# New turns for the weight places, gate weights split between the last expert products, and filler products in TensorE's waits, in a four-layer decoder

## The chip, the core and the metric

The kernel runs on one core of a Trainium2 chip. The core has a matmul engine (TensorE; PE in the profile, its weight loads PEld), a vector engine (DVE), a scalar engine (ACT), GpSimd (POOL) and a sync engine (SP), which only issues transfers here. They meet through semaphores. SP's transfers go through one hardware queue and are served in the order of issue; POOL has a software queue of its own. Both use the core's 16 DMA engines. The metric is the device time of one execution in microseconds.

## What is computed

Four post-norm layers over 256 rows of 1024 float32 values:

```python
for i in range(DEPTH):                       # mixers: conv, retention, sgu, conv
    mix = (_short_conv_mixer, _retention_mixer, _sgu_mixer)[i % 3](x, ...)
    x = _layer_norm(ALPHA * x + mix, ln_g[i, 0], ln_b[i, 0])
    ffn = _moe(x, router_w, router_b, moe_w_gate[i], moe_w_up[i], moe_w_down[i])
    x = _layer_norm(ALPHA * x + ffn, ln_g[i, 1], ln_b[i, 1])
    emb = p[i] @ ple_w_proj[i]
    gate = sigmoid(x @ ple_w_gate[i] + ple_b_gate[i])
    x = x + gate * emb
```

`_moe` routes each row to 2 of 16 experts (gate and up 1024x512, down 512x1024). All experts are loaded, and each works on at most 64 gathered rows; where an expert has more, a general path (`If(crowded > 0)`) makes further rounds. With these inputs it isn't entered.

## The kernel before, in words

**Slots.** All weights arrive as 1 MB slots, [128, 2048] float32. Mixer, embedding and gate weights ("raw" slots, `A["slots"]`) are multiplied in three parts: ACT rounds a slot into `w_hi` (`split_slot`), DVE writes the rest in place as `w_lo`, and TensorE multiplies hi by hi, lo by hi and hi by lo (lines 516 to 518). There are 6 raw places and 4 high places; `split_behind(used)` splits slots up to `used + 4`. The two row tiles of x are t = 0 and 1. A slot of a rows product is 12 matmuls for one tile.

**Experts.** A layer has 96 expert slots (`STREAM`), 12 for each pair of experts, k = 0 to 95. They are multiplied unsplit (line 875). They lie in 16 places that come free after the mixer (raw, high, four of the work area, and those of the norm and bias parameters), and two used once. `expert_places` says which place each k takes; SP issues in that order and waits for each place's last reader (line 430). The places between the first 18 and the last 14 are spread evenly between a place's first and last use.

**End of the experts.** The last pair's down products are slots 92 to 95. Their two halves of y go from PSUM through ACT (`save_y`, the rounded part) and DVE (the rest), and TensorE puts them back into rows (line 885). DVE adds and normalizes tile 0 (`add_rows`, `layer_norm`: lines 1385 to 1435), TensorE transposes it (line 527), ACT and DVE save the transpose in two parts, and TensorE starts on the four gate slots: slots 0 to 2 of tile 0, then tile 1's transposes, slot 3, and tile 1. Each engine runs its own list in the written order, so `split_behind` between two steps makes the later step wait for the splits. `stop` bounds how far it may go.

**Route.** `route` on TensorE mixes the embedding's products (`embed`, 12 for a tile) with the 24 small router products (`logit`) and then waits for DVE to choose. **Convolution.** In layers 0 and 3 DVE weighs four quads (t, q) and ACT and DVE split each; the output rows product needs quad (t, 0) for slots 0 and 1 and (t, 1) for slots 2 and 3. **Clock.** `keep_running(n, bank)` makes n bfloat16 products of constants whose result nobody reads.

## Time and profile before

| | us |
|---|---|
| median of 3 runs | 1759.38 (1757.26 to 1762.88) |
| the profiled execution, device time | 1758.18 |
| its span in the profile | 1756.3 |
| TensorE busy | 1648.1 (94%) |
| DVE busy, ACT busy | 721.5 (41%), 469.0 (27%) |
| moved by DMA | 547.98 MB, mean 312 GB/s |

The chain of work that ended last is PE 75%, DVE 13%, DMA 8%, ACT 3%. Matmuls overlap, so TensorE's busy share is high even where it isn't at its peak. PEclk 1.00 is TensorE's full clock (2.4 GHz), 0.50 the lower level (1.2 GHz). Layer 0 runs its experts from 143 to 356 us of the span and its gate from 368 us; the other layers repeat this from 622, 1117 and 1499 us.

### The profile page before, as it was taken

What the parts mean: (1) busy time and instruction counts of PE and PEld (TensorE: products, weight loads), DVE (VectorE), ACT (ScalarE), POOL (GpSimd) and SP (SyncE); (2) the same over time, 40 slices, a digit from 0 to 9 for tenths busy, and PEclk for the clock granted to TensorE, in tenths of its full rate; (3) what the DMA queues carried; (4) which work ended last, traced back from release to release, by engine and by line L of the source; (5) the groups of instructions that cost most, each with busy time, mean ns of one, the idle gap of its engine ahead of it and who ended that gap; (6) DMA issues with size and microseconds to landing.
All of it is one profiled execution on the core that took longest, in us unless ns stands there. A gap on an engine that the chain in (4) does not pass through costs nothing.

```text
span 1756.3 us, 18018 instructions
## 1 busy us (share of the span) xinstructions
PE 1648.1 (94%) x7628; PEld 989.4 (56%) x7628; DVE 721.5 (41%) x1060; ACT 469.0 (27%) x549; POOL 16.8 (1%) x34
## 2 busy tenths in 40 slices
PE   7999999879999999998799999999987999999986
PEld 5874443358777743432588778544324877434325
DVE  4572111174757721111856656311117566111117
ACT  4531111044443311111444343211103451111112
POOL 0000000000000000000000000000000000000000
PEclk9989999989999999999899999999998998999998
DMA  7487999955443899999565346999995567899991
GB/s 292 177 359 302 421 420 422 419 215 190 163 189 112 354 398 421 421 421 420 211 250 195 145 172 275 408 401 420 421 420 226 197 245 307 330 422 421 421 420 56
DMA packets 77468, 547.98 MB, mean 312 GB/s; under 512 B 8640, under 2 KB 8640, under 8 KB 12608
## 3 DMA queue, kind: packets, MB, share of 16 engines
q1 hardware_dynamic: 73584, 530.95, 74.5%
q0 software_dynamic: 3792, 15.73, 2.4%
q8 instruction: 67, 1.10, 0.2%
q14 instruction: 25, 0.20, 0.0%
HBM read 545.60 MB, written 1.05 MB: 311 GB/s over the span
## 4 chain that ended last, share of the span: by engine, by line
PE 75%; DVE 13%; DMA 8%; ACT 3%; issue 1%; SPq 0%; DVEq 0%; ACTq 0%
PE psum L875 33%; PE psum L516 10%; PE psum L518 9%; PE psum L517 9%; DMA raw<-in_slots 8%; PE psum L867 4%; DVE w_lo L1360 4%; PE psum L885 3%; PE psum L527 3%; ACT w_hi L1071 2%; PE psum L802 1%; DVE work_r L1360 1%; DVE x L1428 1%; DVE stats L1386 1%; DVE x L1385 1%
## 5 line engine op out<-in xcount | busy, mean ns | idle before, releaser
L1360 DVE TENSOR_TENSOR w_lo<-raw,w_hi 128x2048 fp32r<-128x2048 f32 x120 | 271.5, 2287 | 163.7 <-ACT w_hi L1071 163.5
L516 PE MATMUL psum<-w_hi,xT_hi 128*128 128x512 f32 x704 | 283.3, 402 | 16.3 <-DVE w_lo L1360 9.5
L517 PE MATMUL psum<-w_lo,xT_hi 128*128 128x512 f32 x704 | 278.4, 395 | 0.0
L518 PE MATMUL psum<-w_hi,xT_lo 128*128 128x512 f32 x704 | 278.3, 395 | 0.0
L1071 ACT ACTIVATE w_hi<-raw 128x2048 fp32r<-128x2048 f32 x120 | 225.2, 1909 | 137.9 <-PE psum L518 102.0
L1360 DVE TENSOR_TENSOR work_r<-psum,work_r 128x512 fp32r<-128x512 f32 x84 | 56.6, 689 | 366.8 <-ACT work_r L1071 366.8
L1071 ACT ACTIVATE work<-psum 128x512 f32<-128x512 f32 x152 | 89.4, 599 | 413.2 <-PE psum L518 206.9
L875 PE MATMUL psum<-raw,xg 128*64 128x512 f32 x784 | 183.3, 598 | 0.0
L516 PEld LDWEIGHTS psum<-w_hi,xT_hi 128*128 128x128 f32 x704 | 135.1, 192 | 50.3 <-DVE xT_lo L1360 9.6
L518 PEld LDWEIGHTS psum<-w_hi,xT_lo 128*128 128x128 f32 x704 | 134.7, 191 | 29.0
L517 PEld LDWEIGHTS psum<-w_lo,xT_hi 128*128 128x128 f32 x704 | 135.3, 192 | 27.8 <-issue 0.2
L1071 ACT ACTIVATE work_r<-psum 128x512 fp32r<-128x512 f32 x84 | 48.4, 597 | 308.2 <-PE psum L875 307.1
L875 PE MATMUL psum<-expert_high,xg 128*64 128x512 f32 x504 | 120.1, 598 | 5.6 <-DMA expert_high<-in_experts 5.6
L875 PE MATMUL psum<-expert_work,xg 128*64 128x512 f32 x472 | 110.3, 597 | 0.0
L875 PEld LDWEIGHTS psum<-raw,xg 128*64 128x64 f32 x784 | 52.2, 136 | 92.6 <-issue 89.7
L516 PE MATMUL psum<-w_hi,work_r 128*128 128x512 f32 x224 | 90.7, 405 | 11.9 <-DVE work_r L1360 7.5
L1071 ACT ACTIVATE xg<-psum 128x512 f32<-128x512 f32 x64 | 38.2, 597 | 222.3 <-PE psum L867 222.3
L518 PE MATMUL psum<-w_hi,work_r 128*128 128x512 f32 x224 | 89.1, 398 | 0.0
L875 PE MATMUL psum<-raw,work 128*64 128x512 f32 x368 | 86.3, 593 | 2.8 <-DMA raw<-in_experts 2.8
L517 PE MATMUL psum<-w_lo,work_r 128*128 128x512 f32 x224 | 88.8, 396 | 0.0
L867 PEld LDWEIGHTS psum<-work_r 128*128 128x128 f32 x512 | 69.6, 201 | 26.8 <-issue 22.7
L867 PE MATMUL psum<-work_r 128*128 128x256 f32 x512 | 76.5, 299 | 2.1 <-DVE work_r L1661 2.1
(153 smaller groups left out, 1484.3 us busy)
## 6 DMA issues: line engine op xcount, KB each, us to landing
raw<-in_experts SPq DMA_DIRECT2D x144, 1024.0 KB, 14.6
raw<-in_slots SPq DMA_DIRECT2D x120, 1024.0 KB, 4.9
expert_work<-in_experts SPq DMA_DIRECT2D x96, 1024.0 KB, 15.1
expert_high<-in_experts SPq DMA_DIRECT2D x96, 1024.0 KB, 16.1
expert_bias<-in_experts SPq DMA_DIRECT2D x20, 1024.0 KB, 12.2
expert_norm<-in_experts SPq DMA_DIRECT2D x20, 1024.0 KB, 15.9
ln_par<-in_ln_g POOLq DMA_DIRECT2D x8, 512.0 KB, 8.2
ln_par<-in_ln_b POOLq DMA_DIRECT2D x8, 512.0 KB, 11.4
```

Of the source, the lines that this page charges most:

```text
L516: mm(out, lhs[0], rhs[0], start=start, stop=False)
L517: mm(out, lhs[0], rhs[1], start=False, stop=False)
L518: return mm(out, lhs[1], rhs[0], start=False, stop=stop)
L527: last = nc.tensor.transpose(psum[:, bank, i * P:(i + 1) * P], c, ident[:, :])
L802: return mm(psum[:, 4, t * NE:(t + 1) * NE], xT[a][:, j, t * P:(t + 1) * P], rw_split[b][:, j, :], start=i == 0, stop=i == 23)
L867: last = mm(psum[:, bank, j * SEQ:(j + 1) * SEQ], x_split[a][:, t, chunk], pick[:, t, Q * SEQ:(Q + 1) * SEQ], start=t + a == 0, stop=t + a ...
L875: last = mm(psum[columns(e), bank, :], lhs(j, e), w[:, 2 * j + e, :], start=start and j == 0, stop=stop and j == 1)
L885: last = mm(psum[:, bank0 + 2 * t + c, :], where[:, t * P:(t + 1) * P], what[i][:, c * NB:(c + 1) * NB], start=start and i == 0, stop=stop ...
L1071: return nc.scalar.activation(dst, src, func)
L1360: return tt(lo, whole, hi.bitcast(F), ALU.subtract)
L1385: link(stt(xs, xs, ALPHA, psum[:, 2 * t + c, :], ALU.mult, ALU.add))
L1386: step(nc.vector.bn_stats(stats[:, t, c, :], xs))
```

## The change

- **Places**: up to k = 77 each expert slot takes the place whose last reader comes first (`min(..., key=last.get)`); from k = 78 (`BORROWED`) only raw, high and work places are used, so the norm and bias places come free at k = 63 and 66. The last places are taken as raw and high in turn.
- **Gate slots**: SP issues all of them after expert slot 95 (before: the first one ahead of slot 95). ACT and DVE split the first two ahead of the last pair's first y half, the third ahead of its second half (before: one ahead of the second half on DVE and of both on ACT), and the fourth before tile 0 is saved. (Before, DVE split gate slot 1 there, and slots 2 and 3 between saving tile 0 and normalizing tile 1.)
- **TensorE's general path** is a register loop over the rounds, in place of three copies of its body.
- **Fillers**: 10 products after the experts, behind the new semaphore `general_done`, 3 after tile 0's transposes, 2 before the wait for the choice. They multiply the constants.
- **Route**: 2 of tile 1's 12 embedding products stand ahead of the router's (before: 4).
- **Convolution**: slot 0 of tile 1 comes second (before: third), and DVE weighs three quads before it splits two.
- **Start**: the identity is loaded alone, the other constants after raw slot 5, tile 1 of x after raw slot 2; POOL's first loads wait.

```diff
@@ expert_places @@
-        ending = [*reversed(raw), *reversed(high), *work]
+        ending = [v for i in (3, 2, 1, 0) for v in (raw[i + 2], high[i])] + [raw[1], raw[0], *work]
...
-        between = [(first[v] + (final.get(v, first[v] + 5 * len(ring)) - first[v]) * i / 5, v)
-                   for v in ring for i in range(1, 5)]
+        last = {place: k for k, place in at.items() if k < n_first and place in ring}
+        for k in range(n_first, EXPERT_SLOTS - len(ending)):
+            at[k] = min((v for v in ring if k < BORROWED or v in ending), key=last.get)
+            last[at[k]] = k
@@ sync @@
-            sp.dma_start(const[:, :], A["const"]).then_inc(s_const, 16)
+            sp.dma_start(ident, A["const"][:, 0:P]).then_inc(s_ident, 16)
...
-                    if n == 1:
+                    if n == 2:
                         load_x(1)
+                    if n == 5:
+                        sp.dma_start(const[:, P:], A["const"][:, P:]).then_inc(s_const, 16)
                 for k in load_order[L]:
-                    if k == EXPERT_SLOTS - 1:
-                        load(L, n_gate)
...
-                for n in range(n_gate + 1, n_gate + (6 if L + 1 < DEPTH else 4)):
+                for n in range(n_gate, n_gate + (6 if L + 1 < DEPTH else 4)):
@@ gpsimd @@
+            pool.wait_ge(slot_full[1], 16)
             pool.dma_start(p_in, ...)
+            pool.wait_ge(weights_used, 4)
             load_norm(0, 0)
@@ tensor, conv_mixer @@
-                pe.wait_ge(gT_ready[L], 2)
-                rows_slot(n, 4, tiled(gT), 0, 0, 1, mix_done)
+                pe.wait_ge(gT_ready[L], 3)
+                rows_slot(n, 4, tiled(gT), 0, 1, 0, mix_done)
                 pe.wait_ge(gT_ready[L], 4)
-                rows_slot(n, 4, tiled(gT), 0, 1, 0, mix_done)
-                for i in range(2, 4):
+                for i in range(1, 4):
                     rows_slot(n, 4, tiled(gT), 0, 0, i, mix_done)
@@ tensor, route: range(4) is range(2), range(4, 12) is range(2, 12), then @@
+                keep_running(2, 7)
@@ tensor, end of experts @@
+                pe.wait_ge(general_done, L + 1)
+                keep_running(10, 5)
                 transpose_tile(3 * L + 2, 0)
+                keep_running(3, 1)
@@ scalar, experts @@
-                split_behind(n_gate - 3)
+                split_behind(n_gate - 2)
                 save_y(PAIRS - 1, 0, 4)
+                split_behind(n_gate - 1)
                 save_y(PAIRS - 1, 1, 7)
@@ vector, experts @@
+                stop[0] = starts[L + 1][2] if L + 1 < DEPTH else n_gate + 4
+                split_behind(n_gate - 2)
                 save_y(PAIRS - 1, 0, 4)
-                stop[0] = ...
-                split_behind(n_gate - 3)
+                split_behind(n_gate - 1)
                 save_y(PAIRS - 1, 1, 7)
@@ scalar, after experts(L) @@
-                split_behind(starts[L][2] - 2)
+                split_behind(starts[L][2])
                 save_tile(3 * L + 2, 0)
-                split_behind(starts[L][2])
@@ vector, after experts(L) @@
+                dve.sem_inc(general_done, 1)
                 dve.wait_ge(ffn_done, T * L + 1)
                 add_rows(0, 1)
                 layer_norm(0, 2 * L + 1)
-                split_behind(n_gate - 2)
+                split_behind(n_gate)
                 save_tile(3 * L + 2, 0)
-                split_behind(starts[L][2])
```

On SP, at the end of layer 0's expert loads, the order was (raw<-in_slots are the gate slots and then the next layer's first two):

```order
L430 DMA expert_norm<-in_experts 128x2048
L430 DMA raw<-in_experts 128x2048 x6
L430 DMA expert_high<-in_experts 128x2048 x4
L430 DMA expert_work<-in_experts 128x2048 x3
L383 DMA raw<-in_slots 128x2048
L430 DMA expert_work<-in_experts 128x2048
L383 DMA raw<-in_slots 128x2048 x5
```

and it is now:

```order
L429 DMA raw<-in_experts 128x2048
L429 DMA expert_high<-in_experts 128x2048
L429 DMA raw<-in_experts 128x2048 x2
L429 DMA expert_work<-in_experts 128x2048 x4
L382 DMA raw<-in_slots 128x2048 x6
```

The first gate slot moved behind the last expert slot; the other five keep their turn.

On ACT, at the end of layer 0's experts (w_hi<-raw is a gate slot's split, work_r<-psum a half of y), before:

```order
L1071 ACTIVATE work<-psum 128x512 x3
L1071 ACTIVATE work_r<-psum 128x512 x2
L1071 ACTIVATE work<-psum 128x512
L1071 ACTIVATE w_hi<-raw 128x2048
L1071 ACTIVATE work_r<-psum 128x512 x2
L1289 TENSOR_LOAD flag
```

and now:

```order
L1075 ACTIVATE work<-psum 128x512
L1075 ACTIVATE w_hi<-raw 128x2048 x2
L1075 ACTIVATE work_r<-psum 128x512
L1075 ACTIVATE w_hi<-raw 128x2048
L1075 ACTIVATE work_r<-psum 128x512
L1295 TENSOR_LOAD flag
```

Three splits now stand ahead of the second half, and two ahead of the first.

On DVE, at the same place (the first row is the half of pair 6, x<-x,psum is `add_rows` of tile 0), before:

```order
L1360 TENSOR_TENSOR work_r<-psum,work_r 128x512 x2
L1360 TENSOR_TENSOR w_lo<-raw,w_hi 128x2048
L1360 TENSOR_TENSOR work_r<-psum,work_r 128x512
L1385 SCALAR_TENSOR_TENSOR x<-x,psum 128x512
L1386 BN_STATS stats<-x 128x6
```

and now:

```order
L1365 TENSOR_TENSOR work_r<-psum,work_r 128x512
L1365 TENSOR_TENSOR w_lo<-raw,w_hi 128x2048 x2
L1365 TENSOR_TENSOR work_r<-psum,work_r 128x512
L1365 TENSOR_TENSOR w_lo<-raw,w_hi 128x2048
L1365 TENSOR_TENSOR work_r<-psum,work_r 128x512
L1390 SCALAR_TENSOR_TENSOR x<-x,psum 128x512
```

Two splits moved ahead of the first half of the last y, and one stands between the halves.

## Rows read from the trace of the kernel before

**Rows 1.** The page, part 4: shares of the chain that ended last.

```profile
PE 75%; DVE 13%; DMA 8%; ACT 3%; issue 1%; SPq 0%; DVEq 0%; ACTq 0%
```

**Rows 2.** Windows: stretch, length, busy of each engine, PEclk, DMA share, GB/s.

```profile
160.00:330.00 170.00, 169.58 (x808) 66.58 (x806) 25.97 (x47) 21.50 (x36) 1.57 (x3) 1.00 1.01 421
```

**Rows 3.** SP's issues of k = 20 and 21 (start, length), and the microseconds to landing.

```profile
149.05 0.33 SPq L430 DMA_DIRECT2D expert_work<-in_experts  x1
...
expert_work<-in_experts SPq DMA_DIRECT2D x1, 1024.0 KB, 8.0
...
157.73 0.33 SPq L430 DMA_DIRECT2D raw<-in_experts  x1
...
raw<-in_experts SPq DMA_DIRECT2D x1, 1024.0 KB, 4.8
```

**Rows 4.** Timeline, layer 0's end: start, length, instruction [idle before <- releaser].

```profile
351.72 1.91 ACT L1071 ACTIVATE w_hi<-raw 128x2048 fp32r<-128x2048 f32 x1 [6.74 <-DMA raw<-in_slots]
...
354.23 1.94 PE L875 MATMUL psum<-expert_work,work 128*64 128x512 f32 x8 [1.58 <-DMA expert_work<-in_experts]
...
356.95 0.69 DVE L1360 TENSOR_TENSOR work_r<-psum,work_r 128x512 fp32r<-128x512 f32 x1
...
359.41 0.69 DVE L1385 SCALAR_TENSOR_TENSOR x<-x,psum 128x512 f32<-128x512 f32 x1 [0.45 <-PE psum L885]
...
364.77 1.97 PE L527 MATMUL psum<-const,x 128*128 128x128 f32 x8 [5.89 <-DVE x L1435]
365.30 2.29 DVE L1360 TENSOR_TENSOR w_lo<-raw,w_hi 128x2048 fp32r<-128x2048 f32 x1
...
368.24 0.79 PE L516 MATMUL psum<-w_hi,xT_hi 128*128 128x512 f32 x1 [1.50 <-DVE xT_lo L1360]
...
369.21 4.49 DVE L1360 TENSOR_TENSOR w_lo<-raw,w_hi 128x2048 fp32r<-128x2048 f32 x2 [0.43 <-ACT w_hi L1071]
...
373.62 0.68 DVE L1385 SCALAR_TENSOR_TENSOR x<-x,psum 128x512 f32<-128x512 f32 x1
...
380.29 1.32 PE L527 MATMUL psum<-const,x 128*128 128x128 f32 x8 [1.02 <-DVE x L1435]
```

**Rows 5.** Timeline of TensorE in layer 0's gate: every third matmul, twice.

```profile
369.68 0.63 PE L516 MATMUL psum<-w_hi,xT_hi 128*128 128x512 f32 x1
...
370.96 0.63 PE L516 MATMUL psum<-w_hi,xT_hi 128*128 128x512 f32 x1
...
377.07 0.39 PE L516 MATMUL psum<-w_hi,xT_hi 128*128 128x512 f32 x1
...
377.75 0.39 PE L516 MATMUL psum<-w_hi,xT_hi 128*128 128x512 f32 x1
```

**Rows 6.** Windows, as Rows 2: layer 0's gate, and layer 3's convolution.

```profile
363.50:373.80 10.30, 7.53 (x21) 5.97 (x22) 9.73 (x10) 4.79 (x4) 0.00 (x0) 0.50 0.17 71
1449.00:1452.30 3.30, 3.30 (x9) 2.52 (x9) 3.30 (x2) 0.00 (x0) 0.00 (x0) 0.50 1.02 427
```

**Rows 7.** TensorE's waits, 86 to 96 us, then 1440 to 1460: total, times, longest.

```profile
PE psum L516 <- DVE w_lo L1360: 0.9, 1, 0.9
...
PE psum L516 <- DVE w_lo L1360: 2.4, 1, 2.4
```

**Rows 8.** Timeline of TensorE in the route of layers 0 and 1.

```profile
118.84 1.90 PE L533 MATMUL psum<-const 128*128 128x512 bf16 x8
...
137.61 0.42 PE L847 MATMUL psum<-chosen,const 128*128 128x32 f32 x1
...
615.01 0.41 PE L847 MATMUL psum<-chosen,const 128*128 128x32 f32 x2 [1.71 <-DVE chosen L1636]
```

**Rows 9.** Timeline of the start.

```profile
10.16 1.91 ACT L1071 ACTIVATE w_hi<-raw 128x2048 fp32r<-128x2048 f32 x1 [2.46 <-DMA raw<-in_slots]
...
14.54 0.76 PE L516 MATMUL psum<-w_hi,xT_hi 128*128 128x512 f32 x1 [7.47 <-DVE w_lo L1360]
...
22.75 0.50 PE L516 MATMUL psum<-w_hi,xT_hi 128*128 128x512 f32 x1 [0.53 <-DVE w_lo L1360]
```

More of the change, by code:

```diff
@@ L830, in route @@
                 pe.wait_ge(mix_read, L + 1)
-                for i in range(4):
+                for i in range(2):
                     embed(1, i)
@@ L841, in route @@
                 last.then_inc(logits_done, 1)
-                for i in range(4, 12):
+                for i in range(2, 12):
                     embed(1, i)
+                keep_running(2, 7)
                 pe.wait_ge(chosen_ready, L + 1)
@@ L1002, in experts @@
                     o = over[L]
-                    for r in range(ROUNDS):
-                        pe.wait_ge(o["pick"], (T + 1) * (r + 1))
+                    with pe.Fori(0, ROUNDS) as r:
                         with pe.Fori(0, PAIRS) as p:
-                            i = PAIRS * r
+                            pe.wait_ge(o["pick"], (T + 1) * r + (T + 1))
                             wait_over(pe, L, "vector", "weighed", r, p)
@@ L1028, in experts @@
                             wait_over(pe, L, "scalar", "hT", r, p)
-                            pe.wait_ge(o["full"], 16 * (3 * i + 3) + 48 * p)
+                            pe.wait_ge(o["full"], 48 * PAIRS * r + 48 * p + 48)
                             for c in range(2):
@@ L1460, in conv_mixer, with weigh_quad @@
                 dve.wait_ge(dve_step, steps[0])
-                for k in range(4):
+                def weigh_quad(k):
                     t, q = divmod(k, 2)
@@ L1716, in experts @@
                 save_y(PAIRS - 2, 1, 6)
+                stop[0] = starts[L + 1][2] if L + 1 < DEPTH else n_gate + 4
+                split_behind(n_gate - 2)
                 save_y(PAIRS - 1, 0, 4)
-                stop[0] = starts[L + 1][2] if L + 1 < DEPTH else n_gate + 4
-                split_behind(n_gate - 3)
+                split_behind(n_gate - 1)
                 save_y(PAIRS - 1, 1, 7)
```

34 lines of the change are left out of this document (20 added, 14 removed).

## The prediction, made before the changed kernel had run

> **What bounds the kernel.** I read the chain of waits first: three quarters of it is TensorE and 8% is DMA [rows 1]. The windows then show where that 8% lies. From 160 to 330 us the DMA engines are full at 421 GB/s and TensorE's idle is 0.4 us [rows 2]; it was ahead when the stretch began and uses its lead up. A 1 MB slot takes 1.049 MB / 421 GB/s = 2.49 us to arrive. At the end of the stage TensorE starves: the last expert slot is multiplied the moment it lands, at 354.2, after 1.58 us of idle [rows 4]. So an expert stage ends when its transfers end, and the time there is moved by three things only: idle of the transfers at its head, megabytes ahead of the last slot, and the chain behind it. Everywhere else TensorE's order and its clock decide.
>
> **Start.** TensorE's first product waits until 14.54, because ACT gets slot 0 only at 10.16 [rows 9]. Ahead of that slot stand 330 KB of constants and POOL's 256 KB. From tile 0's landing (about 5.0) to slot 0's is 5.1 us, where the slot alone takes 2.49, so POOL's transfer and what goes with it cost 2.6; the constants cost some 0.6 net of the identity. Slot 0 then lands near 6.9 and the product starts near 11.3: 3.3 us. The wait of 0.53 at 22.75 goes too, since slot 2 now stands ahead of tile 1. Term: -3.8. Were POOL's load only worth its bytes (0.6 us), it would be -1.9; were slot 1's cold stretch to shorten as well, -5.
>
> **Convolution, layers 0 and 3.** Slot 1 waited for its `w_lo`, 0.9 and 2.4 us [rows 7]. Slot 0 of tile 1 needs no new slot and its quad is ready, so it fills both. The third weighing falls into DVE's wait for ACT. In layer 3 the idle of 2.4 is followed by 3.4 us at the lower clock [rows 6]; with the gap closed half of it, 1.7, goes. Term: -0.9 - 2.4 - 1.7 = -5.0, or -3.3 if the clock falls anyway.
>
> **Route.** Two embedding products fewer stand ahead of the router's. In layers 1 and 2 the choice is late by 1.71 us [rows 8] and TensorE gains 0.5, but the last expert slot's landing doesn't depend on it there (its transfers are back to back from before the route), so I count 0. In layers 0 and 3 the clock is low and TensorE comes to the choice without idle, at 137.61 [rows 8]. The same 12 products and two fillers now stand ahead of it: 8 fillers took 1.90 at the full clock [rows 8], so two take 0.5, or 0.85 at the lower one. The loads of the stage hang on the first expert product there. Term: 2 x 0.55 = +1.1; from 0 to +1.7.
>
> **Places.** In layer 0 SP issues k = 20 at 149.05, which lands 8.0 later at 157.1, but k = 21 only at 157.73, and it lands 4.8 later at 162.5 [rows 3]. It waited for the raw place's reader, k = 6; the new rule gives it the place read by k = 4, free before 154. So 5.4 - 2.5 = 2.9 us without a transfer disappear, and as the engines are full from there on, every later landing comes 2.9 sooner. The same pattern is there once in each other layer (issues at 632.11, 1153.28 and 1513.18): 1.3, 0.9 and 3.1. Call this g; the sum is 8.3. Near the end the new rule shortens distances between a place's uses to 9, but the queue then holds far more than SP's 5 us of latency, so I cost that at nothing. It would cost if the queue ran dry. The norm and bias parameters' 1.5 MB go earlier; they stay ahead of the last slot, so nothing changes for it.
>
> **End of the experts, four times.** Taking the first gate slot from ahead of slot 95 lets that land 2.49 + g earlier. But ACT now waits for gate slots 0 and 1 before it saves the first half of y, and for slot 2 before the second. They are served behind slot 95. The total ahead of gate slot 1 is unchanged: it lands at 354.2 + 2.5 - g. From there: ACT 1.91, DVE 2.29 (the split), 0.69 (half of y), 2.29, 0.69 and small gaps, 8.0 us to the second half; and 1.77 more to the add, as from 357.64 to 359.41 before [rows 4]. The add thus comes 2.5 + 9.75 = 12.2 after 354.2 where it came 5.2 after: +7.0 - g. Queued behind ACT's wait are both halves of y; TensorE's put-back, tile 0's normalization and its transposes wait for them.
>
> What comes back: counted from the add, the first gate product starts 8.8 later as before (one split still stands ahead, 365.30). Tile 1's transposes came 20.9 later, with TensorE waiting 1.02, since its normalization started only at 373.62, behind two splits of 4.49 [rows 4]. Those are gone. The normalization is ready after 16.1, and TensorE's 36 matmuls decide: at 0.68 us for three [rows 5] 8.2 us, so 17.0. That gives back 3.8. Term: 4 x (7.0 - 3.8) - 8.3 = +4.5.
>
> **Clock at the gate.** Before, the clock is at the lower level from 363.5 to 373.8 [rows 6], after 5.89 us of idle, and three matmuls take 1.28 instead of 0.68 [rows 5]: 2.5 us lost in the product. Now TensorE idles longest ahead of the first half of y (some 7 us), so the clock will fall there. The ten fillers behind `general_done` start about with the add. At the lower clock they take 4.3 us and end a microsecond before the transposes. The loss is between 0 and 2.5 per layer; I take 0.5, nearer to none, since products now run ahead of the gate where TensorE stood idle before. Term: +2.0.
>
> By the Trainium skill ("TensorE: Matmul & The Clock Gate", "HAM oscillation — how this bites in real kernels") an idle between groups of matmuls throttles the array, and the next group starts cold every time. The trace agrees for the 5.89 us gap; taken alone it would have every gate product cold as before, which is the first rival below.
>
> **The sum.** -3.8 - 5.0 + 1.1 + 4.5 + 2.0 = -1.2 us. The register loop lies in a branch that isn't taken; `general_done` costs nothing while tile 0's normalization (5.4 us from the add to the transposes) covers it. The profiled execution took 1758.18 (its span 1756.3 and 1.9 around it), 1.2 below the median. On the median: 1758.2.
>
> **Rivals.**
> - *The splits cost y and the clock isn't won back* (slower). The place is the gate product; it decides where the clock that the fillers raise has fallen again at the product, or they don't raise it. For it: the clock stayed low through tile 0's transposes and until 373.8. Against: nothing ran ahead of them then, and fillers do now. Price 4 x 2.5 = 10 instead of 2: 1766.
> - *The places win nothing* (slower), because the short distances at the end leave the queue dry for as long as the head gained: g = 0, 1766.5. For it: 9 instead of 14 slots. Against: landings trail issues by nearly 30 us there.
> - *More is won on TensorE's side*: start -5, route 0, no cold gate product at all, 2 us less of the last terms: 1752 to 1753. For it: each bound is open. Against: all must go together.
> - *Splits come free*: the gate slots land between the last products after all, y isn't delayed, and the add comes 1.6 + g earlier in each layer; but then the two splits are worth nothing more. -14.7 - 7.7 = -22.4: 1737. Against: SP's queue serves in order, and it is full [rows 2].
>
> **Chances.** Forecast 0.5, cold gate products 0.2, no gain of the places 0.08, more on TensorE's side 0.16, free splits 0.06. A measurement tells 0.3%, 5.3 us, from no change. Faster by that: 0.06, most of 0.16, and the low tail of the forecast, 0.27. Slower: the two slow rivals give 1766 and more, 0.28 less the part that stays under 1764.7, with the forecast's upper tail 0.26. Same: 0.47. Range: with every bound low (-5, -5, 0, +4.5, 0) 1754, and with all high (-1.9, -3.3, +1.7, +4.5, +10) 1770; I take 1750 to 1768, which leaves out the last rival.
>
> **What would show it.** Right: the first product near 11 us; no wait for `w_lo` in the convolutions; DMA share 1 from 155 us on; ACT waiting for gate slots (DMA) right before both halves of y; DVE's add 4 us later in layers 0 and 3 and 6 in layers 1 and 2, counted from the first expert product; no wait of tile 1's transposes. Wrong: expert slots starving earlier than k = 86 by more than a few tenths, w_lo of gate slot 3 on the chain, or the lower clock through the whole gate product.

## The result, and the profile after

The changed kernel takes 1751.9 us (median of 7 runs, 1749.1 to 1753.3), the kernel before 1759.4 (1757.3 to 1764.8): ratio 0.9939, 95% interval 0.9922 to 0.9955. The forecast was 1758.2 and "no change"; it is faster by more than a measurement is uncertain. The profiled execution took 1752.1 (span 1750.3 against 1756.3). Medians of the kernel before vary between 1759.4 and 1762.5 from one group of runs to the next. I compare edits of the changed kernel by their own medians and give the ratio to the kernel before beside them; by the ratios the differences come out up to 3.4 us otherwise, so one of 2 or 3 us says little by its time alone, and I look for it in the trace. Edits of the kernel before (8, 10, 15) are compared by the ratio.

Chain of waits of the changed kernel, shares by engine [rows 1]: transfers and DVE have taken a larger part.

```profile
PE 76%; DMA 10%; DVE 10%; ACT 2%; issue 1%; DVEq 0%; SPq 0%; ACTq 0%
```

Timeline of TensorE at the start (start, length, instruction, [idle before <- releaser]). It answers to [rows 9]: 11.66 for 14.54.

```profile
11.66 0.77 PE L517 MATMUL psum<-w_hi,xT_hi 128*128 128x512 f32 x1 [4.90 <-DVE w_lo L1365]
```

SP's issue of k = 21 in layer 0 and its time to landing [rows 3], then the windows behind it (stretch, length, busy us of PE, PEld, DVE, ACT, POOL, PEclk, DMA share, GB/s):

```profile
147.33 0.33 SPq L429 DMA_DIRECT2D expert_work<-in_experts  x1
...
expert_work<-in_experts SPq DMA_DIRECT2D x1, 1024.0 KB, 5.9
```

```profile
156.00:200.00 44.00, 44.00 (x212) 18.20 (x214) 5.98 (x10) 6.57 (x11) 0.00 (x0) 1.00 1.00 409
200.00:250.00 50.00, 50.00 (x241) 20.18 (x238) 7.81 (x14) 6.57 (x11) 0.00 (x0) 1.00 1.01 421
```

The gap at k = 21 is gone but for 0.5 us, but up to 200 us the engines move 409 GB/s where 421 were forecast: 44 x 12/421 = 1.3 us are lost again. They are lost between 160 and 170 us (366 GB/s at a DMA share of 0.98), with the engines busy; why isn't shown.

Layer 0's end, timeline of ACT, TensorE and DVE [rows 4]:

```profile
346.47 1.91 ACT L1075 ACTIVATE w_hi<-raw 128x2048 fp32r<-128x2048 f32 x1 [9.26 <-DMA raw<-in_slots]
348.96 1.91 ACT L1075 ACTIVATE w_hi<-raw 128x2048 fp32r<-128x2048 f32 x1 [0.58 <-DMA raw<-in_slots]
...
353.85 2.08 PE L886 MATMUL psum<-work_r 128*128 128x512 f32 x4 [7.25 <-DVE work_r L1365]
...
358.52 3.11 PE L534 MATMUL psum<-const 128*128 128x512 bf16 x10
363.83 1.32 PE L528 MATMUL psum<-const,x 128*128 128x128 f32 x8 [2.20 <-DVE x L1440]
...
367.30 0.50 PE L517 MATMUL psum<-w_hi,xT_hi 128*128 128x512 f32 x1 [1.50 <-DVE xT_lo L1365]
...
375.58 1.03 PE L528 MATMUL psum<-const,x 128*128 128x128 f32 x8
...
358.47 0.69 DVE L1390 SCALAR_TENSOR_TENSOR x<-x,psum 128x512 f32<-128x512 f32 x1 [0.55 <-PE psum L886]
```

ACT waits for gate slots ahead of y (9.26 us for slot 0, 0.58 for slot 1), and TensorE stands 7.25 us. From the add (358.47) to tile 1's transposes it is 17.1 us instead of 20.9. The clock [rows 6] is low earlier now, and full in the gate product:

```profile
349.90:360.10 10.20, 5.53 (x12) 2.95 (x13) 9.35 (x10) 5.76 (x5) 0.00 (x0) 0.50 0.70 289
363.50:373.80 10.30, 8.46 (x40) 6.50 (x41) 9.88 (x21) 1.20 (x2) 0.00 (x0) 1.00 0.01 2
```

### The profile page after: what moved, and what is told of

It is laid out like the page before. It is cut to its first block, busy times and chain, and to the rows that moved or that the text cites. A ratio compares the mean times of both kernels' runs of the same rounds, so it can differ in the third digit from the quotient of the medians.

```text
span 1750.3 us, 18145 instructions
## 1 busy us (share of the span) xinstructions
PE 1655.2 (95%) x7688; PEld 987.3 (56%) x7688; DVE 720.8 (41%) x1060; ACT 468.4 (27%) x549; POOL 16.9 (1%) x34
## 3 DMA queue, kind: packets, MB, share of 16 engines
q8 instruction: 66, 1.08, 0.2%
## 4 chain that ended last, share of the span: by engine, by line
PE 76%; DMA 10%; DVE 10%; ACT 2%; issue 1%; DVEq 0%; SPq 0%; ACTq 0%
PE psum L876 32%; PE psum L517 11%; PE psum L519 10%; PE psum L518 10%; DMA raw<-in_slots 6%; PE psum L868 4%; DMA raw<-in_experts 3%; DVE w_lo L1365 3%; PE psum L886 3%; PE psum L528 2%; ACT w_hi L1075 2%; PE psum L802 1%; PE psum L810 1%; DVE work_r L1365 1%; DVE x L1433 1%
## 5 line engine op out<-in xcount | busy, mean ns | idle before, releaser
L517 PE MATMUL psum<-w_hi,xT_hi 128*128 128x512 f32 x704 | 278.9, 396 | 12.7 <-DVE w_lo L1365 6.4
L518 PE MATMUL psum<-w_lo,xT_hi 128*128 128x512 f32 x704 | 274.8, 390 | 0.0
L876 PE MATMUL psum<-expert_work,xg 128*64 128x512 f32 x504 | 117.6, 599 | 0.0
L886 PE MATMUL psum<-work_r 128*128 128x512 f32 x256 | 75.5, 438 | 36.2 <-DVE work_r L1365 36.2
L886 PEld LDWEIGHTS psum<-work_r 128*128 128x128 f32 x256 | 49.2, 204 | 71.7 <-DVE work_r L1365 38.9
## 6 DMA issues: line engine op xcount, KB each, us to landing
expert_norm<-in_experts SPq DMA_DIRECT2D x16, 1024.0 KB, 13.4
```

The costliest lines, as they stand in the source:

```text
L517: mm(out, lhs[0], rhs[0], start=start, stop=False)
L518: mm(out, lhs[0], rhs[1], start=False, stop=False)
L876: last = mm(psum[columns(e), bank, :], lhs(j, e), w[:, 2 * j + e, :], start=start and j == 0, stop=stop and j == 1)
L886: last = mm(psum[:, bank0 + 2 * t + c, :], where[:, t * P:(t + 1) * P], what[i][:, c * NB:(c + 1) * NB], start=start and i == 0, stop=stop ...
```

## Experiments

Each is an edit of the changed kernel unless it says otherwise. First the four parts of the end of the expert stage, then y first, then the parts ahead of it.

**1. Without the thirteen extra products.**

```
-                pe.wait_ge(general_done, L + 1)
-                keep_running(10, 5)
                 transpose_tile(3 * L + 2, 0)
-                keep_running(3, 1)
```

> The changed kernel without its thirteen extra products on the constants at the end of each expert stage and without the semaphore in front of them; all else is kept. Theory A (the clock at the gate was won by these products; my prediction had priced what is left of the loss at 2.0 and the trace after shows none of it): the granted clock falls in the 5 us without a product before tile 0's transposes, the gate product's first half runs at the lower level as in the kernel before (1.28 us for three matmuls against 0.68), 2.5 us per layer, so tile 1's transposes come 19 to 20 us after the add and not 17.1, and the time is 1751.9 + 10 = 1762. Theory B (the products that now run between the two halves of y keep the clock up by themselves): 1752, tile 1's transposes still 17.1 after the add.

Measured 1758.8 (1755.6 to 1761.0), ratio 0.9986 (0.9974 to 0.9999): 6.8 slower than the changed kernel. Timeline and window of layer 0's gate:

```profile
367.81 0.79 PE L517 MATMUL psum<-w_hi,xT_hi 128*128 128x512 f32 x1 [1.50 <-DVE xT_lo L1362]
...
377.67 1.03 PE L528 MATMUL psum<-const,x 128*128 128x128 f32 x8
```

```profile
363.50:373.80 10.30, 7.95 (x27) 6.41 (x28) 9.98 (x19) 1.19 (x2) 0.00 (x0) 0.63 0.01 2
```

The product starts cold. From the add to tile 1's transposes it is 18.7, 19.9, 18.9 and 20.0 us by layer. Theory A, 1.6 to 2.9 a layer.

**2. The route's order of before** (four embedding products ahead of tile 1's router products, no two extra ones).

```
-                for i in range(2):
+                for i in range(4):
                     embed(1, i)
...
-                keep_running(2, 7)
```

> The changed kernel with the route of the kernel before: four embedding products of tile 1 ahead of its router products and no two extra products ahead of the choice. The start of the program and the convolution stay new, so the route begins at the same time as in the changed kernel. Theory A (my prediction's term of +1.1 was right, and the earlier first expert product in layers 0 and 3 comes from where the clock happened to fall and rise, since everything before it begins 5 us sooner): undoing it gives 0.55 us in layers 0 and 3 and nothing else, 1751.9 - 1.1 = 1750.8; from the first transposes of tile 0 in the route of layer 0 to the first expert product it is 19.8 us against 20.36 in the changed kernel. Theory B (the route's new order itself wins the 1.4 and 0.7 us that the traces show in place of a loss): 1751.9 + 2.1 = 1754.0, with 21.7 us from those transposes to the first expert product as in the kernel before.

Measured 1754.5 (1752.8 to 1759.0), ratio 0.9962 (0.9946 to 0.9979): 2.6 slower. By the time it is theory B: my sign was wrong. But layer 0's first expert product doesn't move (137.16), as neither theory had it; counted from the layer's beginning, layer 3's comes 0.9 later, and at the end of the stage layer 1's add comes 1.3 later and layer 2's 0.7 sooner.

**3. Gate slots transferred and split as before** (the splits behind tile 0's normalization too, on ACT and DVE).

```
+                    if k == EXPERT_SLOTS - 1:
+                        load(L, n_gate)
...
-                split_behind(n_gate - 2)
                 save_y(PAIRS - 1, 0, 4)
-                split_behind(n_gate - 1)
+                split_behind(n_gate - 3)
                 save_y(PAIRS - 1, 1, 7)
```

> The changed kernel with the gate slots as in the kernel before: slot 0 of the gate is transferred ahead of the last expert slot, one split between the two halves of y and the others behind tile 0's normalization. The rule for the places and the extra products stay new. Theory A (my prediction's step: the splits cost 7.0 us at the add and give back 3.8 later): the add comes 5.2 us after the last expert slot lands, that is at about 351.6 in layer 0 against 358.5; tile 1's transposes come 20.9 later, at 372.5 against 375.6; 3.1 us per layer, 1751.9 - 12.4 = 1739.5. Theory B (what the splits win back is more than that, because the array now stands idle for 3.9 us between the gate products of tile 0 and of tile 1, and the clock falls in tile 1's half, 2.5 us per layer): 1739.5 + 10 = 1749.5. Theory C (the splits come free, since the end of the stage is set by the transfers of the gate slots anyway): 1752.

Measured 1746.2 (1746.1 to 1748.0), ratio 0.9915: 5.7 faster, between A and B. The add comes at 351.60 and tile 1's transposes at 371.96, as A says; but then the clock falls:

```profile
371.96 1.31 PE L530 MATMUL psum<-const,x 128*128 128x128 f32 x6 [3.08 <-DVE x L1442]
```

```profile
372.70:376.10 3.40, 3.40 (x11) 2.82 (x12) 1.38 (x2) 1.15 (x2) 1.05 (x2) 0.50 0.52 184
```

**6. Experiment 3 with 14 products in that wait** (`keep_running(14, 5)` ahead of tile 1's transposes).

> The kernel with the gate slots as before (the third experiment), and 14 more products on the constants between the third slot of tile 0 in the gate product and the transposes of tile 1, where TensorE waits 3.07 us for DVE. Theory A (the third experiment was 6.7 us slower than its first theory said because the clock falls in that wait, and tile 1's half takes 13.3 to 13.8 us where it takes 11.8 in the changed kernel): the halves take 11.8 again, 1746.2 - 6.8 = 1739.4. Theory B (the missing time is lost elsewhere: in what DVE or the transfers do): 1746, or slower by what the 14 products delay the transposes (3.8 us at the full clock against the 3.07 waited: 0.7 in each layer, 1749).

Measured 1743.2 (1742.7 to 1745.8), ratio 0.9896: 3.0 of the 6.8 came back. Tile 1's half takes 12.1 us in layers 0 to 2 instead of 13.4 to 13.7, so theory A holds for the clock. Most of what is missing lies in layer 1, in experiment 3 too: the gate product starts 11.0 us after the add and not 8.8, since the extra products ahead of it begin late, behind a wait that none of my theories had.

```profile
832.77 1.06 PE L536 MATMUL psum<-const 128*128 128x512 bf16 x2 [5.29 <-issue]
```

**8. The kernel before with the thirteen products, and 10. with the register loop as well.**

```
+                pe.wait_ge(general_done, L + 1)
+                keep_running(10, 5)
                 transpose_tile(3 * L + 2, 0)
+                keep_running(3, 1)
```

> The kernel before with one edit of the change alone: ten extra products behind the general path and three behind tile 0's transposes at the end of each expert stage. Theory A (my prediction's reading: the lower clock costs 2.5 us in each gate product, so lifting it gives 10): 1759.4 - 10 = 1749. Theory B (in the kernel before DVE's two splits hold tile 1's transposes until 20.9 us after the add, and TensorE already waited 1.02 us there, so a faster first half only lengthens that wait to 3.5 us; the products win nothing without the moved splits): 1759.4, tile 1's transposes still 20.9 us after the add. Theory C (as B, and the longer wait lets the clock fall in tile 1's half, as in the third experiment, 1.7 us per layer): 1766.

> The kernel before with the extra products of the eighth experiment and the register loop, nothing else. Theory A (the loop lets the extra products begin with the add, the gate product of tile 0 runs at the full clock; but DVE's two splits hold tile 1's transposes until 20.9 us after the add, so 3.6 us of idle stand there, and the clock falls in tile 1's half as in the third experiment): the gate product 8.8 us after the add, tile 1's transposes 20.9 us after it, and tile 1's half 13.3 instead of 12.1, 1759.4 + 4 x 1.2 = 1764. Theory B (the loop cures the eighth experiment and the clock is won in full): 1759.4 - 10 = 1749. Theory C (the loop has nothing to do with it): 1775 as in the eighth experiment.

Measured for 8: 1775.0 (1772.1 to 1776.3), ratio 1.0074 (1.0056 to 1.0092), and for 10: 1768.4 (1765.4 to 1774.7), ratio 1.0028 (1.0014 to 1.0042). The same products that win 7 us on the new splits lose 13 and 5 on the old ones. TensorE in layer 0 of experiment 8:

```profile
363.68 3.39 PE L533 MATMUL psum<-const 128*128 128x512 bf16 x9 [5.41 <-issue]
...
381.54 1.97 PE L527 MATMUL psum<-const,x 128*128 128x128 f32 x8 [4.16 <-DVE x L1438]
```

```profile
358.30:363.60 5.30, 0.00 (x0) 0.13 (x2) 4.38 (x15) 0.20 (x1) 0.00 (x0) 0.93 1.02 420
```

Two things. TensorE stands 5.41 us behind the branch over the general path with nothing that it waits for, 5.48, 5.43 and 3.05 in the other layers. And tile 1's transposes wait for DVE at the end (theory B), with the clock falling in the wait (C): tile 1's half takes 13.5 to 14.3 us instead of 12.1, 7.4 us in the four layers. But B had them 20.9 us after the add still, and they come after 22.7, 22.9, 24.0 and 20.4: DVE's two splits stand behind its save of tile 0's transposes, and these are late by the wait at the branch. That is another 6.5 us, and the two sums make up the 14.0 us between the profiled spans. With the loop TensorE waits 0.58 and 0.66 us for DVE's semaphore in layers 0 and 2, and stands 3.96 and 3.14 with nothing to wait for in layers 1 and 3; by its time, 10 comes nearest to theory A (1764).

**9. The changed kernel with the general path written out.**

```
-                    with pe.Fori(0, ROUNDS) as r:
+                    for r in range(ROUNDS):
```

> The changed kernel with TensorE's general path written out for its three rounds, as in the kernel before, in a branch that isn't taken in this run. Theory A (seen in the eighth experiment: TensorE's first product behind that branch starts only 5.4 us after the last product ahead of it, with nothing that it waited for in the profile; the register loop makes the branch short, and without it the ten extra products begin 5 us late and hold tile 0's transposes up): the extra products begin at 363.9 in layer 0 instead of 358.5, tile 0's gate product 2.5 to 3.5 us later than now, 1751.9 + 12 = 1764. Theory B (my prediction's step: code in a branch that isn't taken costs nothing): 1752, the extra products at 358.5.

Measured 1751.6 (1748.8 to 1754.5), ratio 0.9927: no difference, theory B by the time. Theory A, which I had read off experiment 8, falls as it stands: the wait behind the branch is there in all four layers (1.68, 1.34, 1.40 and 1.81 us), but short.

```profile
359.57 1.46 PE L534 MATMUL psum<-const 128*128 128x512 bf16 x3 [1.68 <-issue]
```

```profile
357.90:359.50 1.60, 0.00 (x0) 0.00 (x0) 1.50 (x5) 0.00 (x0) 0.00 (x0) 0.50 0.00 0
```

What differs from experiment 8 is the last column: no transfers, against 420 GB/s. The granted clock differs too (0.50 against 0.93), but the shorter wait is the one at the lower clock.

**15. Experiment 8 with the transfers held back while TensorE passes the branch.**

```
+                    if n == n_gate + 2:
+                        sp.wait_ge(general_done, L + 1)
                     load(L, n)
```

> The kernel of the eighth experiment (the kernel before with the extra products, general path written out) in which SP holds gate slot 2 and what follows it back until DVE has passed the general path, so that the DMA engines are empty from about 356.7 in layer 0 while TensorE passes the branch at 358.3. Theory A (TensorE's code behind the branch is fetched by the same DMA engines, and stands behind the 1 MB slots when these run at 421 GB/s): the idle of 5.4 us ahead of the first extra product falls below 2 us in each of the first three layers, the product of tile 0 runs warm, and the time is 1775 less some 3 us per layer and plus what the late slots cost, 1762 to 1768. Theory B (the wait belongs to the branch and its length): 5.4 us of idle as before, 1775 or more.

Measured 1763.0 (1761.0 to 1768.3), ratio 1.0015 (1.0001 to 1.0028): 12 faster than experiment 8 by the medians, 10 by the ratios, theory A.

```profile
363.69 1.82 PE L535 MATMUL psum<-const 128*128 128x512 bf16 x4 [2.31 <-issue]
```

```profile
361.40:363.60 2.20, 0.00 (x0) 0.00 (x0) 1.58 (x4) 0.22 (x1) 0.00 (x0) 1.00 0.29 52
```

The idle is 2.3 to 2.6 us in all four layers, a little over the 2 that I had put as the bound.

**4. Both halves of y saved before any gate slot is split; 7. with 18 and 14 extra products; 14. with none.** DVE's side is shown; ACT saves both halves ahead of its splits too, and DVE's later splits go behind tile 0's normalization and its save.

```
-                split_behind(n_gate - 2)
                 save_y(PAIRS - 1, 0, 4)
-                split_behind(n_gate - 1)
                 save_y(PAIRS - 1, 1, 7)
                 dve.wait_ge(put_half, L + 1)
                 add_rows(0, 0)
+                split_behind(n_gate - 3)
```

> The changed kernel with both halves of y saved before any gate slot is split (ACT and DVE), the first split behind the first add, the second behind tile 0's normalization and the other two behind tile 0's transposes; the transfers stay in the new order. The last expert product ends at 346.6 in layer 0 and DVE is idle from 337 to 348.4, so what DVE has to do between that product and tile 1's normalization (two halves of y, four adds, two normalizations, four splits) can begin 2 us sooner. Theory A (this queue of DVE's is what sets the end of the stage): the add of half 1 at 351 to 352 in layer 0 against 358.5, tile 1's transposes at 372 to 373 against 375.6, 2.6 to 3.6 us per layer, 1751.9 - 12 = 1740. Theory B (TensorE has no product for 3 us before tile 1's transposes, and the clock is low in what follows): 2.5 us less per layer, 1750. Theory C (the gate slots' landing sets the end, in whatever order they are split): 1752.

> The kernel that saves y first (the fourth experiment), with 18 extra products instead of 10 ahead of tile 0's transposes and 14 ahead of tile 1's. In the fourth experiment TensorE still waits 4.1 us before tile 0's transposes and 1 to 2 us before tile 1's, at a clock that fell in each of the four layers. Theory A (that low clock is what is left to gain on TensorE, and tile 1's transposes then come when DVE is ready, 20.4 us after the add, and the half behind them takes 11.8): tile 1's half gains 0.3, 1.7, 1.9 and 1 us, 1738.8 - 5 = 1734. Theory B (DVE sets tile 1's transposes in any case, and 14 products hold them up where the clock is low, since they take 6 us there): 1739 to 1743.

> The kernel that saves y first (the fourth experiment) without its thirteen extra products at the end of each expert stage. There the splits and the transfers of gate slots 2 and 3 are still under way when TensorE passes the general path, and the clock fell in all four layers in spite of the products. Theory A (the products win the clock wherever they stand, 1.7 us per layer): 1738.8 + 7 = 1746. Theory B (they win nothing where DVE sets tile 1's transposes and the clock falls anyhow, and their late start behind the branch in layer 1 costs 2): 1738.8 - 2 = 1737.

Measured 1738.8 (1735.2 to 1740.6), 1738.4 (1737.7 to 1740.0) and 1735.0 (1733.0 to 1736.6); ratios 0.9865, 0.9868 and 0.9849 (0.9826 to 0.9873). So 4 comes out as its theory A (1740) and 7 just under its theory B (1739 to 1743): the products added there win nothing. The last has the lowest time of the study, theory B there: the extra products lose 3.7, though the runs of 4 and 14 overlap. It isn't clearly faster than the old end (13 below, 1736.7, ratio 0.9856). Its layer 0:

```profile
356.55 1.97 PE L528 MATMUL psum<-const,x 128*128 128x128 f32 x8 [7.53 <-DVE x L1436]
360.01 0.80 PE L517 MATMUL psum<-w_hi,xT_hi 128*128 128x512 f32 x1 [1.50 <-DVE xT_lo L1361]
371.55 1.32 PE L528 MATMUL psum<-const,x 128*128 128x128 f32 x8 [1.50 <-DVE x L1436]
```

```profile
360.00:363.40 3.40, 3.39 (x8) 2.71 (x9) 3.40 (x3) 0.00 (x0) 0.00 (x0) 0.50 0.02 5
```

Tile 1's transposes come at 371.55, 4 us before the changed kernel's, although TensorE stood 7.5 us and the gate product begins at the lower clock: DVE decides there, not TensorE. They come 20.4 us after the add in every layer of 14, and in 4 as well but for layer 1 (20.7). What 4 loses lies behind them: tile 1's half takes 13.5 and 13.7 us in its layers 1 and 2, where TensorE had waited 3.04 and 1.89 us for DVE, and 12.1 in all layers of 14, where it waited 1.1 to 1.5. The stretch behind tile 1's transposes in layer 1, in 4 and then in 14:

```profile
850.40:853.80 3.40, 3.40 (x13) 2.80 (x12) 1.74 (x3) 1.20 (x2) 1.05 (x2) 0.50 0.43 129
```

```profile
848.70:852.10 3.40, 3.40 (x19) 2.73 (x20) 2.55 (x4) 1.20 (x2) 1.05 (x2) 1.00 0.35 114
```

**5. The places' rule of before.**

```
-        ending = [v for i in (3, 2, 1, 0) for v in (raw[i + 2], high[i])] + [raw[1], raw[0], *work]
+        ending = [*reversed(raw), *reversed(high), *work]
...
-            at[k] = min((v for v in ring if k < BORROWED or v in ending), key=last.get)
...
+        at.update(zip(range(n_first, EXPERT_SLOTS - len(ending)), [v for _, v in sorted(between)]))
```

> The changed kernel with the rule for the places of the kernel before; all else new. Theory A (my prediction's term: 2.9, 1.3, 0.9 and 3.1 us without a transfer at k = 21 are all gained at the last landing): 1751.9 + 8.3 = 1760.2, last expert slots landing 10.8 us less early than the 10.23 of layer 0 and so on. Theory B (the traces of before and after: counted from the first expert product in layers 0 and 3 and from the layer's start in layers 1 and 2, and less the 2.49 of the gate slot, the last expert slot lands only 1.3, 1.5, 1.4 and 1.3 us earlier, since k = 24, 26 and 29 now land up to 1 us late where no slot did before): 1751.9 + 5.5 = 1757.4. Theory C (the places win nothing at all, the rival of the prediction): 1752.

Measured 1757.0 (1755.1 to 1759.0), ratio 0.9967: the rule is worth 5.0 here, theory B.

**11. The start, and 12. the convolution's order of before.**

```
-            sp.dma_start(ident, A["const"][:, 0:P]).then_inc(s_ident, 16)
+            sp.dma_start(const[:, :], A["const"]).then_inc(s_const, 16)
...
-            pool.wait_ge(slot_full[1], 16)
```

```
-                pe.wait_ge(gT_ready[L], 3)
+                pe.wait_ge(gT_ready[L], 2)
+                rows_slot(n, 4, tiled(gT), 0, 0, 1, mix_done)
+                pe.wait_ge(gT_ready[L], 4)
                 rows_slot(n, 4, tiled(gT), 0, 1, 0, mix_done)
...
-                for k in range(3):
+                for k in range(4):
                     weigh_quad(k)
```

> The changed kernel with the start of the kernel before: all constants and POOL's 256 KB ahead of slot 0, tile 1 ahead of slot 2. Theory A (my prediction's term): 1751.9 + 3.8 = 1755.7, the first product at 14.5, the convolution's first gap at 88.1. Theory B (what the later stages see of it is the place where the clock falls in the route; layer 0's first expert product then moves by other than 3.8): the gap at 88.1 as well, but the first expert product at 137.2 + 3.8 + 1.4 = 142.4, so 1757.

> The changed kernel with the convolution's order of the kernel before (DVE weighs quads 0 and 1, saves them, then 2 and 3; TensorE takes slot 1 of tile 0 ahead of slot 0 of tile 1). Theory A (my prediction's term): the waits of 0.9 and 2.4 us for w_lo come back and in layer 3 the lower clock behind the second, 1751.9 + 5.0 = 1756.9. Theory B (the clock at that place hangs on more than the wait, and stays up in layer 3): 1751.9 + 3.3 = 1755.2.

Measured 1754.4 (1751.9 to 1755.5) and 1758.5 (1753.3 to 1762.1); ratios 0.9943 (0.9928 to 0.9957) and 0.9973. The start is worth 2.4 (A had 3.8), the convolution 6.6 (A had 5.0). By the ratios the start is worth only 0.7; in the traces TensorE's first product comes 2.7 later in experiment 11, and layer 0's add 2.9. In experiment 12 layer 3 waits 2.42 again and its route begins 4.3 later; in layer 0 the wait of 0.89 costs 0.8 at the route, and the last router product comes 2.2 later.

**13 and 16. The whole group at the end of the expert stages taken back** (3 and 1 together, general path written out, which are the edits shown there); **17. the places as well; 18. the route as well, places kept.** The profile is that of 16, the same program.

> The changed kernel with its whole end of the expert stage taken back: gate slots and their splits as in the kernel before, no extra products there, TensorE's general path written out. Start, convolution, route and places stay new. Theory A (my prediction's sum: that group costs 4.5 + 8.3 for the places, which stay, + 2.0 = 14.8): 1751.9 - 14.8 = 1737.1. Theory B (the parts undone one by one: start 2.4, convolution 6.6, route 2.6 and places 5.0 are worth 16.6 together, so what is left of the change costs 16.6 - 7.5 = 9.1): 1742.8. Theory C (splits and extra products undone one by one add up, -5.7 + 6.8): 1753.

> The thirteenth experiment's program once more, for its profile. Its time 1736.7 again. Theory A (the forecast's step for the places: the last landing comes 2.9, 1.3, 0.9 and 3.1 us earlier): from the first expert product to the last slot's landing 210.56 - 2.9 = 207.7 in layer 0. Theory B (as in the changed kernel, 1.3 us): 209.3. For the route: the lower clock in layers 0 and 3 lasts as long as in the changed kernel, 10.2 and 13.7 us, against 13.7 and 17.1 in the kernel before.

> The thirteenth experiment's kernel with the rule for the places taken back as well, so that start, convolution and route alone are new. Theory A (the forecast's term for the places): 1736.7 + 8.3 = 1745.0, and what is left, start, convolution and route, is worth 1759.4 - 1745 = 14.4 where the forecast had 7.7. Theory B (the places are worth what they are in the changed kernel): 1736.7 + 5.0 = 1741.7. Theory C (the missing 7 us are the places', because the last expert slot's landing sets the end here): 1736.7 + 15 = 1752.

> The thirteenth experiment's kernel with the route taken back as well, so that start, convolution and places alone are new. Theory A (the forecast's +1.1): 1736.7 - 1.1 = 1735.6. Theory B (as in the second experiment, where the route's order was worth 2.6): 1739.3. Theory C (the missing 7 us are the route's): 1736.7 + 5.6 = 1742.3.

Measured: 13, 1736.7 (1735.6 to 1737.0), ratio 0.9856; 16, 1736.7 (1735.0 to 1742.2), ratio 0.9872 (0.9854 to 0.9891); 17, 1744.6 (1743.7 to 1746.4), ratio 0.9910; 18, 1741.3 (1739.8 to 1741.8), ratio 0.9886. So the group costs 15.2 (theory A of 13; 11.8 to 14.6 by the two ratios), the places are worth 7.9 (A of 17) and the route 4.6 where the last expert slot sets the end (18 lies between its theories B and C, nearer to C). From layer 0's first expert product to the last landing it is 209.1 us in 16: theory B, and 1.5 less than in 17. Layer 0's end in 16 is that of [rows 4], 8.1 earlier:

```profile
346.15 1.94 PE L878 MATMUL psum<-expert_work,work 128*64 128x512 f32 x8 [1.59 <-DMA expert_work<-in_experts]
...
356.69 1.97 PE L530 MATMUL psum<-const,x 128*128 128x128 f32 x8 [5.89 <-DVE x L1440]
...
372.21 1.32 PE L530 MATMUL psum<-const,x 128*128 128x128 f32 x8 [0.93 <-DVE x L1440]
```

The route of layer 3, the stretch at the lower clock: before, then 18 (old order), then the changed kernel and 16 (new order).

```profile
1479.70:1496.80 17.10, 16.83 (x66) 15.03 (x66) 8.99 (x30) 2.46 (x6) 0.00 (x0) 0.50 0.77 302
```

```profile
1465.50:1482.50 17.00, 16.71 (x69) 15.21 (x68) 7.52 (x29) 2.69 (x6) 0.00 (x0) 0.50 0.77 300
```

```profile
1472.90:1486.50 13.60, 13.60 (x52) 11.75 (x51) 5.26 (x18) 1.96 (x5) 0.00 (x0) 0.50 0.71 275
```

```profile
1461.60:1471.80 10.20, 9.99 (x36) 8.57 (x36) 4.16 (x17) 0.38 (x2) 0.00 (x0) 0.50 0.82 311
```

TensorE's 32 products behind the choice, in 18 at the lower clock and in 16 at the full one:

```profile
1476.77 6.63 PE L869 MATMUL psum<-work_r 128*128 128x256 f32 x32 [0.23 <-DVE work_r L1674]
```

```profile
1473.64 4.10 PE L870 MATMUL psum<-work_r 128*128 128x256 f32 x32 [0.63 <-DVE work_r L1675]
```

## Why the prediction was wrong, step by step

**Start, -3.8: measured -2.4** by experiment 11, -2.9 at the first product. POOL's share was put a little too high: the product was to start at 11.3 and starts at 11.66. Within its bounds.

**Convolution, -5.0: measured -6.6.** Both waits are gone. At the route's start in layer 3 it is 4.3, where 4.1 was forecast. What is more comes in layer 0's route: with the convolution's old order the clock stays low there for 13.7 us, as before, and for 10.2 in the changed kernel.

**Route, +1.1 (0 to +1.7): measured -2.6, and -4.6 without the new end.** This is the step that failed. I priced two products moved and two added at their durations, at a given clock, and took all behind the choice as given. Up to the choice that held: from the route's first transposes to the choice it is 0.3 to 0.8 us longer with the new order in layers 0 and 3 (2 against the changed kernel, 18 against 16), where +0.55 was forecast. Behind it it failed: from the choice to the first expert product of layer 3 it is 7.5 and 8.7 us with the old order (2, 18) and 6.0 and 5.6 with the new, because there the clock is back at its full level while TensorE makes the 32 products behind the choice (4.10 us for 6.63). The stretch at the lower clock in that route is 17.1 us long in three of the six traces with the old order (before, 2, 18), 13.7 in two (8, 15) and 20.5 in one (10); with the new order it is 10.2 in eleven of thirteen and 13.7 in two. Four of the six have the convolution's old order too, so only 2 and 18 show the route's order alone. What is shorter of the stretch is worth half its length.

The 4.6 isn't all the route's. From the layer's beginning to its first expert product, layer 3 takes 130.4 us in 18 and 126.7 in 16, but 1.4 of that lies ahead of the route, where 18 has a fall of the clock that 16 hasn't; and another 1.6 is lost in 18 in tile 1's half of layer 0, also to the clock. Whether the order has to do with these two, one profile of each can't tell. In layers 1 and 2 the choice is no longer waited for, but the end of the stage gains at most 0.5 between 18 and 16, as forecast. That the order shortens the slow stretch is shown, by two pairs of profiles; why it does isn't.

**Places, -8.3: measured -7.9 in front of the old end, but -5.0 in the changed kernel.** Counted from the first expert product (layers 0 and 3) or the layer's beginning (1 and 2), and less the gate slot's 2.49, the last expert slot lands 1.3, 1.5, 1.4 and 1.3 us earlier. In front of the old end (17 against 16) it is 1.5, 1.6, 4.5 and 1.8 in place of 2.9, 1.3, 0.9 and 3.1: the sum agrees (9.3 by these landings, 7.9 by the medians), but of the layers only layer 1 does, so that is luck. In the changed kernel the gap at k = 21 closed but for 0.5 us, and the 409 GB/s up to 200 us take most of the rest: in layer 0, k = 24, 26, 28 and 29 each land more than a transfer behind the slot ahead, by 2.6 us together, where before only k = 28 did, by 1.35.

**End of the experts, 4 x (7.0 - 3.8).** The add comes 7.0 us later in layer 0, counted from the first expert product and against experiment 16 (221.3 against 214.3), the number of the forecast; 3.8 us come back at tile 1's transposes in every layer, also as forecast. In the other layers the add is 8.0, 9.6 and 7.2 later. Moving the gate slot behind slot 95 was to let that land 2.49 earlier; against 16 it lands 2.3 and 2.1 earlier in layers 0 and 3, 1.3 in layer 1, and 0.3 later in layer 2. There k = 89 lands 1.0 late (layer 1) and k = 92 1.5 late (layer 2), though both had been issued some 20 us before, so it isn't an empty queue; what it is isn't shown.

**Clock at the gate, +2.0: measured about -1.2.** The gate product runs at the full level in all four layers, and tile 1's half takes 11.8 us instead of 12.1. The products do it, as forecast (experiment 1), and I was too careful about how far.

**The sum.** For the end with the clock, and the places kept, the forecast had 12.8 + 2.0 = 14.8; taking all of it back gives 15.2. That is luck in part: the first term was 3.8 too low by the adds, the second 3.2 too high. For the four parts ahead it had -16.0, and they are worth -22.7; of the 6.7 that lie between, the route's term makes 5.7. So 1736.7 was forecast as 1743.4, and the whole change as 1758.2 instead of 1751.9. The likeliest case lost to the rival "more on TensorE's side" (1752 to 1753), which counted no gain of the route, but the places in full and a start of -5. Its number fits by luck.

**What would show it:** the first product near 11, no wait for `w_lo` in the convolutions, a DMA share of 1, ACT's waits for gate slots 0 and 1 ahead of the first half, and tile 1's transposes without a wait were there. Ahead of the second half ACT splits slot 2 without waiting. The add was to come 4 us later in layers 0 and 3 and 6 in layers 1 and 2, from the first expert product, and came 5.5 later in 0 and 3, 6.5 in 1 and 5.1 in 2.

**The register loop, 0:** confirmed in the changed kernel (experiment 9), though not for the reason given, that a branch which isn't taken is free. A jump over a path that isn't entered has a price, 1.3 to 1.8 us in experiment 9, which here falls into a stretch without transfers.

**The extra products elsewhere.** With y first they lose 3.7, behind the old splits 9.5 (3 against 13), in the kernel before 13 (8). The traces show where. Where DVE sets tile 1's transposes, an earlier gate product only makes TensorE wait longer for them, and tile 1's half behind that wait runs in part at the lower clock: 3.0 us over four layers in 4 against 14, 6.1 in 3 against 16, 7.4 in 8 against before. Ahead of each of these halves TensorE had waited 1.9 to 4.5 us; not every such wait does it (3.07 in layer 0 of 15, and the half took 12.1). The late start behind the branch adds the rest in layer 1 of 3 (3.1 us) and in 8.

Not settled: why the route's order shortens the slow stretch.

## What to carry to other kernels

Price a moved product by what it does to the stretch of low clock around it, not by its own duration: here products worth half a microsecond decided over 1.5 to 3.1 us behind the choice of one layer. Work that is put into a critical queue because "the engine will wait there anyway" has to be compared with what that queue could have done in the wait: here y first, with the splits behind it, is 13 us faster than the changed kernel, and 17 without the extra products. And undo parts together as well as one by one: the extra products won 7 us, or lost 4, 9.5 or 13, by what stood around them.

## What the runs showed of the hardware

TensorE's code comes through the DMA engines while the kernel runs: the page after has a queue of kind "instruction" with 66 packets and 1.08 MB. Behind the branch over the general path TensorE stood 5.4 us with transfers at 420 GB/s, 2.3 to 2.6 with them held back, and 1.7 where the engines were empty (layer 0 of experiments 8 and 9, all layers of 15). In layers 1 and 3 the shorter code of the loop doesn't help: 3.96 and 3.14 (experiment 10).

```profile
q8 instruction: 66, 1.08, 0.2%
```

The window of TensorE's wait in layer 0 of experiment 8 (358.3 to 363.6 us) holds one such packet among the slots' own:

```profile
q1 hardware_dynamic: 302, 2.21, 100.4%
q8 instruction: 1, 0.02, 1.3%
```

So it is for all twelve of these waits in experiments 8, 9 and 15: one packet of 16.4 KB and about 1 us lies in the wait or just ahead of it, and TensorE's next product starts 1.4 to 2.0 us behind its end. Under full transfers (8, layers 0 to 2) the packet starts 2.4 to 2.5 us after the last product ahead of the branch, which is about one slot's 2.49; in 15 it starts 0.2 before that product's end, in 9 0.9 to 1.1 before it. This fits theory A of 15, that the code stands behind the slots. That TensorE waits for this very packet isn't recorded; the order in time is.

By the Trainium skill ("Advanced Engine Details and Errata", "ISA Cache") instructions are held in lines of 16 KB, 256 instructions each, and there are only two lines; it gives 32 KB in all, but 128 KB for TensorE. The 16.4 KB of a packet here agree with the line; how many lines TensorE keeps no run shows.
